# Rotations and forget sums taken off TensorE in two hybrid attention layers

## The reference

```python
def hybrid_layer(h, pos, ...):
    u = rms_norm(h, norm_g)
    dq, dk, dv, dz, fq, fk, fv, fz, f_logit = split(u @ w_in)
    # "d": 4 heads of 2 x 64, q and k are rotated by position
    q1, q2 = diff_qk(dq); k1, k2 = diff_qk(dk)          # each through rope(t, pos)
    p = softmax(causal(q1 @ k1.T * s)) - lam * softmax(causal(q2 @ k2.T * s))
    o_a = rms_norm(p @ v_a, subln_g) * (1 - lambda_init)
    # "f": 8 heads of 64, no rotation, a running sum of log forget gates as bias
    cum = cumsum(log_sigmoid(f_logit + b_forget))        # (8, 272)
    s = q_f @ k_f.T * s + cum[query] - cum[key]
    o_b = softmax(causal(s)) @ v_f
    mixed = concat(o_a * silu(dz), o_b * silu(fz))
    return h + mixed @ w_out
def rope(t, pos):                                        # halves t1, t2 of 32 each
    return concat(t1 * cos - t2 * sin, t2 * cos + t1 * sin)
return rms_norm(h, final_g)[:, 16:]
```

## Time and profile before

| what | value |
|---|---|
| median of 3 runs | 1898.8 us (1897.58 to 1910.72) |
| profiled execution, span from first to last instruction | 1893.8 us |
| hybrid layer 0, first projection to start of product | 1448.0 to 1631.9 us |
| hybrid layer 1, first projection to start of product | 1681.6 to 1857.5 us |
| PE / DVE / ACT / POOL busy over the span | 1788.9 / 843.5 / 413.6 / 57.5 us |
| granted TensorE clock, mean | 0.967 |

### The profile page before, as it was taken

One profiled execution on the slowest core, in us unless ns is written; L12 is line 12 of the kernel. 1 busy time (PEld: TensorE's weight loads), 2 busy tenths in 40 slices (PEclk: granted clock), 3 DMA queues, 4 the chain that ended last, 5 costly groups with the idle time before them and its releaser, 6 DMA issues.

```text
span 1893.8 us, 25538 instructions
## 1 busy us (share of the span) xinstructions
PE 1788.9 (94%) x10478; PEld 1358.7 (72%) x10478; DVE 843.5 (45%) x1790; ACT 413.6 (22%) x1010; POOL 57.5 (3%) x71
## 2 busy tenths in 40 slices
PE   7999989999999999999988999899998999999997
PEld 5777768776587876878766778587886677556774
DVE  3244333744334335444357747434433444324353
ACT  1000022533200002000146412200002253113521
POOL 0200000000000000000003130000000000000000
PEclk9999998999999999999998959999998999999999
DMA  6754554212344544544433300254556762467520
GB/s 225 251 181 142 137 134 134 67 67 81 120 156 136 198 134 134 177 157 161 158 103 105 126 24 1 90 162 150 168 157 102 114 96 84 88 82 106 99 89 22
DMA packets 194168, 232.74 MB, mean 123 GB/s; under 512 B 27028, under 2 KB 175960, under 8 KB 194056
## 3 DMA queue, kind: packets, MB, share of 16 engines
q1 hardware_dynamic: 191584, 224.97, 43.3%
q0 software_dynamic: 1840, 5.12, 0.9%
q10 hardware_dynamic: 632, 1.04, 0.1%
HBM read 230.07 MB, written 1.05 MB: 122 GB/s over the span
## 4 chain that ended last, share of the span: by engine, by line
PE 89%; DVE 5%; ACT 2%; issue 2%; DMA 1%; ACTq 0%; DVEq 0%
PE ps L502 26%; PE ps L275 25%; PE ps L555 15%; PE ps L462 6%; PE ps L516 3%; PE ps L1629 1%; DMA ring<-in_ffn_w_up 1%; PE ps L1464 1%; PE ps L358 1%; PE ps L2148 1%; PE ps L2164 1%; PE ps L2152 1%; PE ps L2178 1%; PE ps L2183 1%; PE ps L1646 1%
## 5 line engine op out<-in xcount | busy, mean ns | idle before, releaser
L275 PE MATMUL ps<-hT,ring 128*128 128x272 f32 (+2 forms) x1504 | 363.9, 396 | 3.6 <-issue 1.3
L275 PEld LDWEIGHTS ps<-hT,ring 128*128 128x128 f32 (+1 forms) x1504 | 280.8, 190 | 65.2 <-issue 8.5
L555 PE MATMUL ps<-ring,arena 128*128 128x512 f32 x704 | 309.4, 592 | 0.0
L555 PEld LDWEIGHTS ps<-ring,arena 128*128 128x128 f32 x704 | 130.4, 190 | 147.3 <-issue 147.3
L502 PE MATMUL ps<-arena 128*128 128x128 f32 x1920 | 222.7, 276 | 0.0
L502 PEld LDWEIGHTS ps<-arena 128*128 128x128 f32 x1920 | 219.4, 193 | 0.0
L502 PEld LDWEIGHTS ps<-hT,ring 128*128 128x128 f32 x1280 | 156.8, 193 | 26.0 <-issue 19.1
L502 PE MATMUL ps<-hT,ring 128*128 128x128 f32 x1280 | 163.6, 276 | 6.4 <-DMA ring<-in_ffn_w_up 6.4
L627 DVE TENSOR_TENSOR arena<-arena,ps 128x256 f32<-128x256 f32 x40 | 16.8, 421 | 256.5 <-ACT arena L591 256.5
L640 DVE TENSOR_TENSOR arena<-arena,ps 128x384 f32<-128x384 f32 x80 | 44.2, 554 | 183.4 <-PE ps L502 183.4
L593 ACT ACTIVATE arena<-arena 128x512 f32<-128x512 f32 x40 | 25.2, 630 | 384.7 <-DVE arena L640 384.7
(11 more groups left out here) (408 smaller groups left out, 2165.7 us busy)
## 6 DMA issues: line engine op xcount, KB each, us to landing
ring<-in_ffn_w_gate SPq DMA_DIRECT2D x44, 1024.0 KB, 5.5
ring<-in_ffn_w_up SPq DMA_DIRECT2D x44, 1024.0 KB, 5.8
ring<-in_ffn_w_down SPq DMA_DIRECT2D x44, 1024.0 KB, 5.0
ring<-in_w_in SPq DMA_DIRECT2D x32, 1024.0 KB, 9.4
ring<-in_ab_w_in SPq DMA_DIRECT2D x12, 1024.0 KB, 5.3
ring<-in_w_out SPq DMA_DIRECT2D x8, 1024.0 KB, 5.0
ring<-in_ab_w_out SPq DMA_DIRECT2D x6, 1024.0 KB, 4.9
ring<-in_c_w_k SPq DMA_DIRECT2D x4, 1024.0 KB, 5.5
```

The source lines that it names most:

```text
L275: last = nc.tensor.matmul(o, l, r, start=(i == 0), stop=(i == len(pairs) - 1))
L555: m = nc.tensor.matmul(ps[:, 2 * t + h, :], hid[:, q % 2, i, t * P:(t + 1) * P], slot2(s0 + 3 * q + 2)[:, i, h * 512:(h + 1) * 512], start ...
```

## The change

1. Rotations. PE's 8 matmuls per layer with `rot` go. GpSimd instead issues 4 DMAs per dq or dk tile from `fmh` to `rth` in SBUF, each 32 partitions, which swap the two halves of every head (a new function `hybrid_pool`). DVE multiplies this by sin, whose constant now carries the sign, one step later than before (at p-2 instead of p-1), and adds as before. Two buffers of `rth` alternate, and GpSimd waits for the sum of the tile before the last.
2. Forget sums. PE's 2 spreading matmuls per "f" unit go. After the scan GpSimd stores the 8 rows of `fl` to DRAM, waits, loads them to all 128 partitions (8 x 272 numbers each, into rows of `gains` not needed any more), waits, and adds the causal mask for each query tile with three or two tensor additions. DVE adds this `bias_of(t)` to the scores in the place of the mask.
3. In layer 1, the projections dq, fq, dz and fz are made for the 256 last positions only (`f_cols`), on PE and in ACT's evictions, and so are dq's rotations.

```diff
@@ hybrid_pe
-                group(f_bank(n)[:, 0:L2], [(slot8(s)[:, k, (p % 2) * P:(p % 2 + 1) * P], hT[:, k, :]) for k in range(KD)])\
+                fc = f_cols(layer, FT[p][0])
+                group(f_bank(n)[:, fc], [(slot8(s)[:, k, (p % 2) * P:(p % 2 + 1) * P], hT[:, k, fc]) for k in range(KD)])\
                     .then_inc(f_ready, 1)
-                if kind in ("dq", "dk"):
-                    pe.wait_ge(f_taken, raw_n[kind, i])
-                    x_turn()
-                    group(ps[:, 7, 0:L2], [(const("rot"), fmh[:, QK[kind] + i, :])]).then_inc(x_ready, 1)
-                elif kind in ("dv", "fv"):
+                if kind in ("dv", "fv"):
...
                         pe.wait_ge(f_taken, raw_n["fk", i])
-                        pe.wait_ge(cum_ready, layer + 1)
...
-                    if kind == "f":
-                        for c in range(2):
-                            m = nc.tensor.matmul(ps[0:r, c, 0:w], ident[0:8, 2 * i + c:2 * i + c + 1].broadcast_to([8, r]),
-                                                 fl[:, 0:w], start=False, stop=True)
@@ hybrid_dve
+                    if kind == "d":
+                        bias = q_mask(t).rearrange("p (o n) -> p o n", o=1).broadcast_to([r, 2, w])
+                    else:
+                        if i == 0:
+                            dve.wait_ge(bias_ready, dve_b())
+                        bias = bias_of(t)[:, 2 * i:2 * i + 2, :]
+                    dlink(dve, nc.vector.tensor_tensor(pr, ps[0:r, 0:2, 0:w], bias, ALU.add))
...
+                if p - 2 in ROT_TILES:
+                    kind, i = FT[p - 2]
+                    fc = f_cols(layer, kind)
+                    n = dve_r()
+                    tmp, raw = rth[:, (n - 1) % 2, fc], fmh[:, QK[kind] + i, fc]
+                    dve.wait_ge(rot_in[(n - 1) % 2], 64 * ((n + 1) // 2))
+                    dlink(dve, nc.vector.tensor_tensor(tmp, tmp, const("sin")[:, fc], ALU.mult))
+                    dlink(dve, nc.vector.tensor_tensor(raw, raw, const("cos")[:, fc], ALU.mult))
+                    nc.vector.tensor_tensor(raw, raw, tmp, ALU.add).then_inc(roped, 1)
@@ new
+        def hybrid_pool(pool, layer):
+            for p in ROT_TILES:
+                kind, i = FT[p]
+                fc = f_cols(layer, kind)
+                n = pool_r()
+                pool.wait_ge(f_taken, 36 * layer + p + 1)
+                if n > 2:
+                    pool.wait_ge(roped, n - 2)
+                for q in range(4):
+                    to, of = slice(32 * q, 32 * q + 32), slice(32 * (q ^ 1), 32 * (q ^ 1) + 32)
+                    nc.gpsimd.dma_start(rth[to, (n - 1) % 2, fc], fmh[of, QK[kind] + i, fc]).then_inc(rot_in[(n - 1) % 2], 16)
+            pool.wait_ge(cum_ready, layer + 1)
+            nc.gpsimd.dma_start(cum_rows[layer], fl).then_inc(cum_in, 16)
+            pool.wait_ge(cum_in, 32 * layer + 16)
+            nc.gpsimd.dma_start(cum_all[:, :, :], cum_rows[layer].rearrange("(o h) n -> o h n", o=1).broadcast_to([P, 8, L2])).then_inc(cum_in, 16)
+            pool.wait_ge(cum_in, 32 * layer + 32)
+            for t in ([T] if layer == 0 else []) + list(range(T)):
+                r, w = u_rows(t), u_width(t)
+                nc.gpsimd.tensor_tensor(bias_of(t), cum_all[0:r, :, 0:w], q_mask(t).rearrange("p (o n) -> p o n", o=1).broadcast_to([r, 8, w]),
+                                        ALU.add).then_inc(bias_ready, 1)
```

More of the change, by code:

```diff
@@ L84, in constants @@
     put("cos", np.tile(np.cos(ang), (4, 1)))
-    put("sin", np.tile(np.sin(ang), (4, 1)))
+    put("sin", np.tile(np.concatenate([-np.sin(ang), np.sin(ang)]), (2, 1)))
     put("pairsel", (i[:, None] // 64) == np.arange(2)[None, :])
@@ L2045, in model_kernel @@
         nlam = lam[:, 0:1]
+        cum_all = gains[:, 4:7, :].rearrange("p a n -> p (a n)")[:, 0:8 * L2].rearrange("p (h n) -> p h n", h=8)
+        bias_1 = gains[:, 0:3, :].rearrange("p a n -> p (a n)")[:, 0:8 * L2].rearrange("p (h n) -> p h n", h=8)
+        bias_0 = more[:, 0:8 * 144].rearrange("p (h n) -> p h n", h=8)
+        cum_rows = [nc.dram_tensor(f"cum_rows{layer}", (8, L2), F32, kind="Internal").ap() for layer in range(2)]
+        bias_m = more[0:META, 1152:1152 + 8 * META].rearrange("p (h n) -> p h n", h=8)
         FT = [(kind, i) for a in "df" for half in range(2) for kind in (a + "q", a + "k", a + "v") for i in (2 * half, 2 * half + 1)]
@@ L2055, in model_kernel @@
         pe_f, act_f, dve_f = Turn(), Turn(), Turn()
-        pe_x, dve_x, act_x2 = Turn(), Turn(), Turn()
+        pe_x, dve_x, dve_r, pool_r, dve_b = Turn(), Turn(), Turn(), Turn(), Turn()
+        ROT_TILES = [p for p, (kind, i) in enumerate(FT) if kind in ("dq", "dk")]
         def f_bank(n):
@@ L2084, in q_cols, with f_cols, bias_of @@
             return slice(0, META) if t == T else slice(META + t * P, META + (t + 1) * P)
+        def f_cols(layer, kind):
+            return slice(META if layer == 1 and kind[1] in "qz" else 0, L2)
+        def bias_of(t):
+            return {T: bias_m, 0: bias_0, 1: bias_1}[t]
         def u_nb(t):
@@ L2202, in hybrid_act @@
                 act.wait_ge(f_ready, n)
-                src = f_bank(n)[:, 0:L2]
+                fc = f_cols(layer, kind)
+                src = f_bank(n)[:, fc]
                 if kind in QK:
-                    nc.scalar.activation(fmh[:, QK[kind] + i, :], src, ACT.Copy, scale=SCR if kind[1] == "q" else 1.0).then_inc(f_taken, 1)
+                    nc.scalar.activation(fmh[:, QK[kind] + i, fc], src, ACT.Copy, scale=SCR if kind[1] == "q" else 1.0).then_inc(f_taken, 1)
                 elif kind[1] == "v":
@@ L2217, in hybrid_act @@
                 if p == 12:
-                    act.wait_ge(x_taken, 17 * layer + 12)
+                    act.wait_ge(x_taken, 9 * layer + 3)
                     alink(act, nc.scalar.activation(fl2, fl, ACT.Abs))
@@ L2279, in hybrid_dve @@
                         dve.wait_ge(pt_ready, n - 3)
-                    msk = qmask[0:META, L2 - P:L2 - P + META] if t == T else qmask[:, L2 - w:]
                     pr = hprob[0:r, b, :, 0:w]
-                    dlink(dve, nc.vector.tensor_tensor(pr, ps[0:r, 0:2, 0:w], msk.rearrange("p (o n) -> p o n", o=1).broadcast_to([r, 2, w]),
-                                                       ALU.add))
-                    nc.vector.tensor_reduce(hstat[0:r, b, 0:2], pr, AX, ALU.max, negate=True).then_inc(sc_masked, 1)
@@ L2333, in hybrid_dve, with q_mask @@
                     nc.vector.tensor_tensor(hmT[:, z, lo:], hmT[:, z, lo:], zraw[:, z, lo:], ALU.mult).then_inc(hm_ready, 1)
+        def q_mask(t):
+            return qmask[0:META, L2 - P:L2 - P + META] if t == T else qmask[:, L2 - u_width(t):]
+        def hybrid_pool(pool, layer):
+            for p in ROT_TILES:
+                kind, i = FT[p]
+                fc = f_cols(layer, kind)
+                n = pool_r()
[14 more added lines that the diff above has]
+                                        ALU.add).then_inc(bias_ready, 1)
         def z_turn(layer, z):
@@ L2379, in _ @@
             rwkv_pool(pool)
+            for layer in range(2):
+                hybrid_pool(pool, layer)
         @block.scalar
```

19 lines of the change are left out of this document (7 added, 12 removed).

## The result

| | before | after |
|---|---|---|
| median | 1898.57 us (4 runs) | 1876.37 us (1871.61 to 1880.09, 4 runs) |
| profiled execution, span | 1893.8 us | 1873.0 us |
| layer 0, first projection to start of product | 183.97 us | 173.45 us |
| layer 1, the same | 175.96 us | 166.26 us |

The ratio of the medians is 0.987 [0.984, 0.991]: 22 us less, where 24.8 were forecast. A second comparison of the same two kernels gave 1879.12 against 1898.59, 0.988 [0.986, 0.991].

A forecast was written before the change was run, and what follows sets the result against it. The prediction took PE, busy 94% of the span, as the bound: 25.8 us removed from PE (7.8 + 14.5 + 3.5) less 1 for the port gave -24.8, so 1898.8 becomes 1874.0 us, range 1868 to 1886.

The forecast's parts named there:

- PE's savings, 25.8 us: Work removed from PE in both hybrid layers: rotations 7.8, forget bias 14.5, layer 1's columns 3.5 us, all on the path.
- L of the rotations: Time from issue to landing of GpSimd's rotation DMAs: 4 to 5 us; above 6.3 a layer loses 2L - 12.6.
- Rival 1: Rotations partly late, landing in 7 to 10 us; at 9, 10.8 us lost, total 1885; chance 0.14.
- The bias in layer 1: Forget sums' way through DRAM and GpSimd before the first "f" unit: hidden, cost 0, bounds 0 to 4 us.
- L1: Landing time of GpSimd's store of the forget sums to DRAM: 4 us, upper bound 6.8.
- L2: Landing time of the forget sums' broadcast back to 128 partitions: 8 us, upper bound 16.
- the prediction's own formula: Layer 1's bias needs 3.7 + L1 + L2, covering two issues and the first add, against 19.2 us available.
- tolerance: Lateness of DVE's bias add that PE bears, needing it only after the next group: some 4 us.
- rival 3: Bias late, DVE then PE stand before first "f" units: up to 4 us, 8 if GpSimd is slower; 1879; chance 0.08.
- The port, 0.5 a layer: GpSimd's adds hold one two-input DVE operation up to 5 us per layer; charged 1 us in all, bounds 0 and 4.
- rival 4: DVE, not PE's records, sets step time, so only steps 0 to 23 gain: 17.7 us, total 1882; chance 0.06.
- all hidden: Main case: the added transfers in both layers delay nothing, total 1870 to 1879 us; chance 0.62.

The follow-up runs named there:

- the kernel with four buffers: Changed kernel with broadcast and adds cut by pairs of heads, and four rotation buffers instead of two, GpSimd issuing: 1871.60 us, ratio 0.984 to before.
- The kernel without the way through DRAM: Changed kernel without the forget sums' store to DRAM and broadcast back; adds read whatever lies there, so output is wrong: 1879.37 us, ratio 0.990 to before.
- the kernel with 16 more of them: Changed kernel with a small store to DRAM, waited for, ahead of each rotated tile's DMAs: 1931.36 us, ratio 1.018 to before.

## Why the prediction was right, point by point

- **PE's savings, 25.8 us.** Right where nothing new waits: the kernel with four buffers is 25.8 us shorter in its two layers, 11.4 in layer 0 (11.6 by the forecast's rows) and 14.4 in layer 1 (14.3), so the tenth itself is luck. The parts: columns 3.4 measured against 3.5; rotations 4.0 against 3.9 in layer 0; the bias 6.7 against 7.6 in layer 0, of which 0.6 is the wait for DVE's held L2321 that this kernel had there, and 6.7 against 6.8 in layer 1 once its wait and the clock of the first two tiles are taken out. Start-to-start distances were the right price.
- **L of the rotations.** "I take 4 to 5": the middle was 3.4, the longest 10.9. The 2.1 estimated from the Trainium skill ("DMA: Bandwidth & Descriptors", Anatomy of one DMA — SWDGE) isn't what the runs gave, though the fastest of 64 pieces took 1.7; the measurement decides. A single L was the weak point: the formula charges nothing up to 6.3 if all landings are alike, while single late ones of 10.9 to 18.9 cost 0 to 2.7 us of waiting in most profiles and 6.15 in one, which with the clock came to 9.9. Rival 1 as a state of the whole layer didn't come. That the changed kernel's first profile had no such wait was luck; its second had one of 1.96.
- **The bias in layer 1: the mis-sized term.** I took L1 = 4 and L2 = 8 and a cost of 0. Measured: 7.7 and 14.2. By the prediction's own formula 3.7 + 7.7 + 14.2 = 25.6 against 19.2, 6.4 late, less 4 of tolerance: 2.4. The formula is a little off in two places that nearly cancel. The landings count from the issue's start, so the two issues are in it twice: from the scan's end to the end of the first add it was 25.0. And the tolerance was 3.0, not 4: DVE's add came 5.9 us later than PE's work asked for, and PE waited 2.91. Then the clock, which the prediction left out: the four pieces from 1767.21 to 1774.58 took 7.37 us, and the same ones in the kernel with four buffers 5.73 (1766.35 to 1772.08), 1.64 more. Together 4.55, of the 4.7 us that divide the two kernels' layer 1. The kernel without the way through DRAM says the same, 4.7 from the third tile on. So this is rival 3's mechanism, inside the bounds of 0 to 4 with its wait and just outside with the clock; the sign named for it, a broadcast of over 12 us, came too.
- **L1 in particular.** The upper bound of 6.8 for the store came from loads of 512 KB, and 8.5 KB took 7.7 us: the bound was no bound.
- **The port, 0.5 a layer.** 0.76 in layer 0, and in layer 1 the 3.38 us hold reached nobody. The mechanism is as named, the hold longer than the "up to 5 us" where adds follow each other (6.54, over the end of one add and the whole of the next). That the engine held back waits for the other's whole instruction, as the Trainium skill has it ("SBUF — State Buffer", Who interferes with whom), the trace bears out for one add: the holds of 5.21 and 3.38 us each end 0.3 us behind one. A hold of 6.42 us over a train of adds is more than that. The 0.5 was right for the changed kernel by where its adds fell; without the way through DRAM the same hold cost 6.2 us.
- **DVE at the gates (rival 4).** It didn't come. PE has no wait on DVE in the gate steps of either layer, and the bias and columns savings of those steps are in the sum. One argument against it was misread: in the trace of before DVE doesn't wait for PE ahead of each such add, not ahead of those at 1604.07 and 1608.80.
- **Sum.** By its number the result lies where the prediction said "all hidden"; by its mechanism not all was hidden, and rival 3 came in part. Forecast -24.8; -22.2 and -19.5 by the medians, -20.8 by the spans, -20.2 by the layers. The whole is right because the loss, some 4.7 us in layer 1 and 1 in layer 0, is small beside the sum, and 1876.4 lies 2.4 us from the forecast; the second comparison's 1879.1 lies 5.1 from it. The 5 us between span and median are not an overhead of each run: a run lies some 1.8 us above its own span (1874.80 and 1873.0 here), the rest is that the profiled execution of before was a short one.

## What to carry to other kernels

Work taken off the bounding engine pays its start-to-start time in full as long as nothing new is waited for, and here that could be reckoned from the trace of before, within some 0.3 us for each part. What can't be reckoned from a median is the tail of small transfers that run beside weight loads: give such a transfer more buffers and an issuer whose time nobody needs, and move nothing important behind its wait in an in-order queue. Price a wait of the bounding engine with the slower clock that may follow it. And before a length is compared between two profiles, look where the difference arises: up to 2.2 us of layer 1's lay in its first two tiles, with the same edit or none.

## What the runs showed of the hardware

- Small transfers in stretches with 1 MB weight loads: pieces of 34 KB landed after 1.7 to 18.9 us, a store of 8.5 KB to DRAM after 7.4 to 10.3 (1.6 to 13.9 in the kernel with 16 more of them), the same 1.1 MB broadcast after 5.9 to 14.2. A quarter of the broadcast took 13.0, 9.0 and 7.6 in layer 1.
- The granted clock after PE's waits was 0.61 after 2.91 us, 0.69 after 3.60, 0.50 and 0.65 after 6.15, 0.50 after 11.49. With the clock these waits came to 4.6, 6.2 and 9.9 us, 1.6 to 1.7 times the wait (the last wasn't reckoned). It was 0.57 after 1.42 in one profile and 1.00 after 1.64 in another.
- The first two tiles of layer 1 ran at a granted clock of 1.00 in seven profiles and at a lower one in six (0.50 to 0.63), with 1.6 to 2.2 us between them, whatever the kernel.
- DVE operations other than those with two tensors in SBUF were held beside GpSimd's adds too. In the fastest kernel a scaling of 16 x 16 elements, which takes 0.22 us in the changed kernel, stood until the adds were over. Here it delayed nobody:

```profile
1545.29 7.37 DVE L2337 TENSOR_SCALAR arena<-arena,small 16x16 f32<-16x16 f32 x1
```

- A rotation's DMA issue on ScalarE took up to 3.2 us, where one on GpSimd took at most 0.64, in the kernel with the extra stores.
